# Later transposes of x's groups, and a smaller zero product, in the opening of a two-layer decoder kernel

## The reference

```python
proj = rms_norm(x, gla_attn_norm) @ gla_w_in          # 256 x 2048 times 2048 x 6160
q, k, v, r, a_low = jnp.split(proj, [...], axis=-1)   # a_low: the last 16 columns
log_a = log_sigmoid(a_low @ w_alpha2 + b_alpha) / 16
```

## Time and profile before

| what | value |
|---|---|
| median of three runs | 2192.73 us |
| the profiled execution's own time | 2192.34 us |
| its span in the trace | 2190.4 us |
| PE busy | 2185.3 us (100%) |
| DVE busy | 1254.1 us (57%) |
| ACT busy | 1058.5 us (48%) |
| POOL busy | 298.8 us (14%) |
| DMA, mean | 205 GB/s |

### The profile page before, as it was taken

How to read it: one execution, slowest core, us unless ns; L and a number is a source line. 1 busy time by engine, 2 the same in 40 slices (tenths; PEclk the granted TensorE clock), 3 DMA queues, 4 the chain that set the end, 5 groups by cost and what they waited for, 6 DMA issues and landing times.

```text
span 2190.4 us, 27314 instructions
## 1 busy us (share of the span) xinstructions
PE 2185.3 (100%) x9722; PEld 1811.2 (83%) x9722; DVE 1254.1 (57%) x1491; ACT 1058.5 (48%) x1432; POOL 298.8 (14%) x595
## 2 busy tenths in 40 slices
PE   9999999999999999999999999999999999999999
PEld 7888888888888888888888888888888888888887
DVE  6666666645555555554566676665555555555443
ACT  6666455444444444444456665554444444444333
POOL 3410334100000000001135333341000000000000
PEclk9999999999999999999999999999999999999999
DMA  8766667676677666666667666677666766666665
GB/s 264 220 188 178 191 203 223 204 216 195 209 205 207 203 204 208 201 199 203 203 208 222 195 206 205 202 224 209 198 210 199 216 194 210 204 211 193 194 192 166
DMA packets 254130, 448.06 MB, mean 205 GB/s; under 512 B 28224, under 2 KB 43040, under 8 KB 254048
## 3 DMA queue, kind: packets, MB, share of 16 engines
q1 hardware_dynamic: 236608, 428.79, 64.8%
q0 software_dynamic: 17264, 18.12, 2.8%
q10 hardware_dynamic: 176, 0.07, 0.0%
HBM read 414.37 MB, written 2.10 MB: 190 GB/s over the span
## 4 chain that ended last, share of the span: by engine, by line
PE 98%; DMA 1%; DVE 0%; POOL 0%; SPq 0%; ACT 0%; issue 0%; DVEq 0%; POOLq 0%
PE acc L671 32%; PE acc L673 32%; PE acc L672 32%; DMA raw<-in_gla_w_in 0%; POOL g_r L614 0%; PE side L946 0%; DMA g_r<-g_r 0%; PE side L782 0%; PE side L817 0%; PE side L960 0%; PE side L944 0%; PE side L962 0%; PE side L961 0%; PE side L832 0%; PE side L831 0%; PE side L833 0%
## 5 line engine op out<-in xcount | busy, mean ns | idle before, releaser
L1389 DVE TENSOR_TENSOR w_lo<-raw,w_hi 128x1024 fp32r<-128x1024 f32 x783 | 952.0, 1223 | 798.9 <-ACT w_hi L1006 794.3
L1006 ACT ACTIVATE w_hi<-raw 128x1024 fp32r<-128x1024 f32 x783 | 825.2, 1059 | 973.2 <-PE acc L673 960.7
L671 PE MATMUL acc<-w_hi,xT 128*128 128x512 f32 x2016 | 786.2, 390 | 0.0
L673 PE MATMUL acc<-w_hi,xT 128*128 128x512 f32 x2016 | 784.4, 389 | 0.0
L672 PE MATMUL acc<-w_lo,xT 128*128 128x512 f32 x2016 | 784.3, 389 | 0.0
L673 PEld LDWEIGHTS acc<-w_hi,xT 128*128 128x128 f32 x2016 | 378.5, 188 | 78.6
L671 PEld LDWEIGHTS acc<-w_hi,xT 128*128 128x128 f32 x2016 | 378.5, 188 | 78.3
L672 PEld LDWEIGHTS acc<-w_lo,xT 128*128 128x128 f32 x2016 | 378.5, 188 | 78.2
L671 PE MATMUL acc<-w_hi,hT 128*128 128x512 f32 x700 | 272.3, 389 | 0.0
L672 PE MATMUL acc<-w_lo,hT 128*128 128x512 f32 x700 | 272.3, 389 | 0.0
L673 PE MATMUL acc<-w_hi,hT 128*128 128x512 f32 x700 | 272.3, 389 | 0.0
(11 more groups left out here) (233 smaller groups left out, 1413.2 us busy)
## 6 DMA issues: line engine op xcount, KB each, us to landing
raw<-in_ffn_w_in SPq DMA_DIRECT2D x352, 512.0 KB, 4.3
raw<-in_ffn_w_out SPq DMA_DIRECT2D x176, 512.0 KB, 4.8
raw<-in_gla_w_in SPq DMA_DIRECT2D x95, 512.0 KB, 4.5
raw<-in_w_kv SPq DMA_DIRECT2D x64, 512.0 KB, 4.5
raw<-in_gla_w_out SPq DMA_DIRECT2D x32, 512.0 KB, 4.6
raw<-in_diff_w_q SPq DMA_DIRECT2D x32, 512.0 KB, 4.8
raw<-in_diff_w_out SPq DMA_DIRECT2D x32, 512.0 KB, 4.6
tok<-scratch SPq DMA_DIRECT2D x352, 32.0 KB, 3.3
```

Source lines behind the costliest of these rows:

```text
L671: nc.tensor.matmul(acc[p][tb][:, :], hi, w_hi[:, slot, j, :], start=(kt + j == 0), stop=False)
L673: last = nc.tensor.matmul(acc[p][tb][:, :], lo, w_hi[:, slot, j, :], start=False, stop=(kt + j == n_kt - 1))
L1006: nc.scalar.activation(w_hi[:, slot, :, :], raw[:, slot, :, :], ACT.Copy).then_inc(hi_done, 1)
L1389: nc.vector.tensor_tensor(w_lo[:, slot, :, :], raw[:, slot, :, :], w_hi[:, slot, :, :].bitcast(F32), ALU.subtract).then_inc(lo_done, 1)
```

## The change

Three edits, all in PE's order. The zero product in `x_first_job` stood between the transposes of the first and the second k-tile and had 256 columns; it now stands behind those of the second, with 128 columns. `x_job(2)` stood ahead of unit 1 and now stands inside it, behind the first four of its eight products with `w_hi`. `x_job(3)`, `x_job(4)` and `x_job(5)` stood ahead of units 1, 2 and 3, and now stand ahead of units 2, 3 and 4. The orders of ACT, DVE, POOL and SP are as they were.

```diff
-            def first_unit(src, kt, n_kt, p, slot, u):
+            def first_unit(src, kt, n_kt, p, slot, u, between=None):
                 pe.wait_ge(hi_done, u + 1)
                 for j in range(UNIT_KT):
                     for tb in range(TB):
                         for part in range(2):
                             nc.tensor.matmul(acc[p][tb][:, :], src[:, part, kt + j, tb * P:(tb + 1) * P], w_hi[:, slot, j, :],
                                              start=(kt + j == 0 and part == 0), stop=False)
+                    if between and j == 0:
+                        between()
                 pe.wait_ge(lo_done, u + 1)
...
                 last.then_inc(x_first_turned, 1)
-                zeros(1)
                 pe.wait_ge(x_second_in, 16)
                 for tb in range(TB):
                     last = nc.tensor.transpose(acc[1][0][:, tb * P:(tb + 1) * P], x[:, tb, P:2 * P], ident)
                 last.then_inc(t_done[0], 1)
+                nc.tensor.matmul(side[1][:, 0:P], g_at[:, 0, 0, :], g_at[:, 0, 1, :], start=True, stop=True)
...
-                    if b == 0 and k == 1:
-                        x_job(2)
-                    if b == 0 and 1 <= k < 4:
-                        x_job(k + 2)
+                    if b == 0 and 2 <= k < 5:
+                        x_job(k + 1)
...
                         very_first_unit(lambda: x_job(1))
+                    elif u == 1:
+                        first_unit(xT, 2, KT, 0, 1, 1, lambda: x_job(2))
                     else:
```

## The result

The changed kernel takes 2197.37 us in the median of 12 runs (2195.38 to 2198.96), the kernel before 2192.73 us in the median of 12 (2191.84 to 2193.11). The ratio is 1.0022, 95% interval 1.0013 to 1.0031: slower, by 4.6 us, where 1.7 us was forecast and 2195.6 was the top of the range. The spread has grown too, from 1.3 us to 3.6 us.

A forecast was written before the change was run, and what follows sets the result against it. L782's start, held by a path over DVE, POOL's moves and ACT, was taken to bound the kernel. The profiled 2192.34 us plus 1.69 gave 2194.03; the median's 0.39 above made it 2194.4 us, range 2192.8 to 2195.6.

The forecast's parts named there:

- The path: Group 4's lo part on DVE, square transposes, POOL's moves, landing, ACT's hi parts, then L782: claimed 1.69 us later.
- the squares' end: DVE's square transposes of groups 6 and 7, queued behind group 4's lo part: end near 20.58 instead of 18.89.
- POOL's first move: First of POOL's 16 moves, waiting for DVE's square transposes: near 21.2 us instead of 19.51.
- The landing: Time POOL's last move takes to land: 5.0 us taken, 2.6 to 5.0 seen, 0.5 more possible.
- Part 4: What PE keeps: it reaches L782 about 0.2 us earlier and waits there about 2.5 us; the saving lies there.
- the third rival: Smaller zero product at the start makes PE's clock rise later in unit 0: +3.8 us, 2196.5 us; chance 0.08.
- signs of being wrong: Squares starting by 18 us, L782's wait not growing, another PE wait behind 40 us.
- The first: Path to L782 has a reserve, so the change keeps what it frees: 2192.0 to 2192.9 us; chance 0.12.
- The second: Moves land quicker and ACT's order decides, +0.7 to +1.0 us: 2193.1 to 2193.7 us; chance 0.15.

The follow-up runs named there:

- e2: The changed kernel with the zero product put back as before, so only the x_jobs moved: 2196.99 us, ratio 1.0020.
- e9: The kernel before with only x_job(4) and x_job(5) one unit later, ahead of units 3 and 4: 2196.89 us, ratio 1.0019.
- e4: The changed kernel with six zero products, read by nobody, ahead of PE's wait for groups 6 and 7: 2195.26 us, ratio 1.0012.
- e10: The changed kernel with four zero products ahead of PE's wait for groups 6 and 7: 2195.25 us, ratio 1.0011.
- e5: The changed kernel with DVE's square transposes of groups 6 and 7 put ahead of group 4's lo part: 2193.46 us, ratio 1.0003.
- e1: The kernel before with the zero product's edit alone (128 columns, behind the second k-tile's transposes): 2192.57 us, ratio 1.0000.
- e6: The changed kernel, but SP sends unit 11's weights only when all 16 moves of groups 6 and 7 have landed: 2195.64 us, ratio 1.0012.
- e3: The changed kernel with x_job(4) put back ahead of unit 2, behind x_job(3): 2193.78 us, ratio 1.0004.

## Why the prediction was wrong

*The path was right.* The direction, the place (L782's start) and the mechanism (DVE's order puts the squares behind group 4) held, and the steps fell close: unit 1 at 10.38 for a forecast 10.55, unit 2 at 14.03 for 14.12, the squares' end 20.49 for 20.58, POOL's first move 21.11 for 21.2. In the timeline of the changed kernel:

```profile
10.38 1.16 PE L683 MATMUL acc<-w_hi,xT 128*128 128x512 f32 x4 [0.36 <-ACT w_hi L1008]
11.38 0.60 PE L737 MATMUL tps<-const,x 128*128 128x128 f32 x4
...
14.03 2.10 PE L683 MATMUL acc<-w_hi,xT 128*128 128x512 f32 x8
...
16.89 0.60 PE L737 MATMUL tps<-const,x 128*128 128x128 f32 x4
```

*The landing was mis-sized.* I took 5.0 us with 0.5 above it as the limit; it was 6.15, and that is 1.13 of the 2.72 us by which L784 is late; the squares are the other 1.60. The range of one execution's rows (2.6 to 5.0, rows 8) was taken for the range of the quantity, though the last move had its maximum and was to go out at another place among the weight loads. In other executions it took 5.16 (e2), 5.22 (e9), 5.54 (e4), 5.86 (e10), 6.28 (e5).

*A term was missing.* Part 4 said that the rest of the saving "lies in this wait" and priced a wait of 2.5 us at its length. It costs more: PE's clock falls in it and stays low for the products behind it, 2.56 us in the profiled execution and 2.1 in the median (e4). I did weigh the clock, as the third rival, but only for the zero product at the start, where nothing happened: the four transposes inside unit 0 last 0.60 us as before, and e1 shows no cost. A rule that bears on it is in the Trainium skill, "TensorE: Matmul & The Clock Gate", in the table of "Why this matters for your kernels": avoid long idle gaps of PE between bursts of products in mid-kernel, since they bring the lower clock. The changed kernel's trace agrees (a wait of 3.41 us, granted clock 0.50); but the page means gaps longer than the wait that I forecast, and e5's fall around 1.84 us isn't covered by it. None of the signs of being wrong that I had named came, for none of them looked at the clock there.

*The rivals.* The first (a reserve at L782) is out: the wait grew from 0.6 to 3.4 us. The second (moves land quicker) went the other way. The third named the right resource in the wrong place: its number, 2196.5 us, is the nearest to the measured one of all four, and that is luck. Forecast and measurement meet again when the term is taken out: e4, the changed kernel with its clock kept up, took 2195.26 us, within the range of 2192.8 to 2195.6; of the 0.9 us above 2194.4 the landing is the likely source (5.54 for 5.0 us in its profiled execution), which the median of runs without traces can't confirm.

## What to carry to other kernels

When work is moved on one engine, read what each engine that consumes it has queued behind it: here four transposes of 0.36 us, moved to a place where PE had time for them, delayed an unrelated step of DVE and with it a path of 20 us. A wait of TensorE can have two prices, its length and the lower clock behind it (here 2.5 and 2.1 us in the medians); when a forecast makes one longer, add the second with a chance, and if the wait can't be avoided, fill it with products that nobody reads.

## What the runs showed of the hardware

The length of the wait alone doesn't decide whether the clock falls, and what else does isn't shown. PE's wait at the gate's products was 1.68 us in e2's profiled execution, 1.67 in e6's and 2.64 in e9's, and the granted clock stayed 1.00; in e5's it was 1.84 us, and the clock fell at about 39.5:

```profile
37.00:39.50 2.50, 0.66 (x5) 0.49 (x5) 1.96 (x8) 1.34 (x2) 0.89 (x2) 1.00 0.96 303
39.50:42.00 2.50, 2.50 (x14) 2.50 (x13) 1.71 (x2) 2.50 (x3) 0.00 (x0) 0.51 0.27 104
```

There PE had already been at work again since 39.01. Of the 12 runs of the changed kernel 11 had a mean clock below 1.000, of e9's 11 runs nine, of e2's eight, of e6's four, of e5's one, of e3's none. And the view of the clock doesn't show the lower level at the start of the program: in rows 9 it reads 1.00 at 5.0 to 6.5 us, where the two passes of a zero product take 0.85 us, 0.43 each, while in e4 twelve of the same passes take 2.75 us, 0.23 each.
